# Query projection on tokens that are only scaled, with the shift's part as a product of its own, in a diffusion layer

## The chip, the cores and the metric

One core of one Trainium2 chip. The metric is the time of one execution in device microseconds, as the median of several runs.

## What is computed

One layer for 384 tokens of width 2048 in float32: 128 context tokens and 256 tokens of a denoising step, each group with its own conditioning vector. Cut to what matters here:

```python
mod = jax.nn.silu(cond) @ p['w_ada'][l] + p['b_ada'][l]           # 2048 x 12288
sh1, sc1, gt1, sh2, sc2, gt2 = jnp.split(mod[:, None, :], 6, axis=-1)
h = _rmsnorm(x, p['g_pre_mix'][l]) * (1.0 + sc1) + sh1
proj = h @ p['w_in'][l]                    # q, k, v, g, lr and the Hyena columns
...                                        # gated linear attention and Hyena, w_out, norm, gate
x = x + gt1 * _rmsnorm(y, p['g_post_mix'][l])
h = _rmsnorm(x, p['g_pre_ffn'][l]) * (1.0 + sc2) + sh2
y = _moe(h, l, p)                          # 16 experts, two for a token
```

`w_ada` is 100 MB. Its first third holds the shift `sh1` and the scale `sc1` that the first projection needs; the other four parts are wanted later.

## The kernel before, in words

All engines run programs written out by hand and tied by semaphores. `take` gives a PSUM bank to a result once the readers of the last one are done, `filled`, `read` and `freed` are its semaphores.

**Loads.** The SP engine issues one DMA for each entry of the list `loads` (L991 to L1002), in order: first sixteen 2 MB blocks of w_ada (128 rows by 4096 columns, shift and scale together), then the halves of w_in and w_out. A block goes into one of three ring slots, from the 17th load on into one of two; before it is issued, SP waits until TensorE has released the slot (`slot_done`). After each load SP issues so many *pieces* of the rest of w_ada (`PIECES_AFTER`, L367), 0.5 MB each as two DMAs, in a ring of four; piece n waits until VectorE has used piece n - 4 (L986). SP works strictly in order, so a load stands behind the pieces ahead of it. The rows of small vectors and the constants are issued by SP behind the first load (L968), the filter MLP's inputs and x by ScalarE's queue (L1215 to L1224), biases, gains, and later the lr and decay weights, masks and filter weights by GpSimd (L1076 to L1102, held at L1083 until the first tile is modulated).

**Start.** TensorE (L411 to L485) turns the small rows, does the first filter product (it waits for the MLP's inputs, L419), then sixteen `ada_step`s (L439), one for each block: eight products of 32 columns of weights by 512, four side by side in the array. Between the last eight it transposes the normalised tokens (`x_turn`, L456), which ScalarE copies into `hT` (L1256). When both sums are there, VectorE adds biases and gains (`mod_row`, L1557), TensorE transposes the two rows (`mod_columns`, L475), and VectorE modulates the 16 tiles of `hT` in 32 operations (L1623).

**Projections.** `project_half` (L487) takes one ring slot (8 row blocks by 512 columns of w_in) and does 8 products for each of 4 or 3 banks. Query (L526) comes first, 64 products of 384 columns, recorded in halves (x128); then the small lr product (L530), the eight decay products (L538), the key (L543), two value and two gate blocks, then six Hyena blocks. The four gated heads of the attention (`gla_head`, L596) are mixed into the second g1 half and the first Hyena blocks.

**The rest of w_ada.** VectorE sums the pieces, weighted by silu(cond), into 16 chunks (`ada_steps`, L1573). `run(n)` does n steps of two operations each; a piece is two steps, a chunk eight pieces. VectorE's program places these steps between its other work. TensorE then sums a chunk over partitions (`ada_sum`, L423, at the places of `ADA_SUMS`, L364), waiting for `chunk_ready`, and VectorE adds it (`mod_chunk`).

## Time and profile before

| what | value |
|---|---|
| median of 3 runs | 1532.09 us (1527.59 to 1532.54) |
| profiled execution, its own time | 1530.56 us |
| its span | 1528.7 us |
| mean granted TensorE clock | 0.965 |
| TensorE products busy | 1379.7 us (90%) |
| VectorE busy | 748.8 us (49%) |
| ScalarE busy | 241.7 us (16%) |
| HBM read and written | 408 MB and 23 MB, 282 GB/s over the span |

The span is the part between the first and the last instruction that the profiler saw; the difference to the execution's own time lies around it. Busy shares are averages over stages with different limits, so the views by stage and the chain of waits are read beside them. A granted clock of 1.00 is 2.4 GHz, 0.50 is 1.2 GHz.

### The profile page before, as it was taken

The numbers are of one execution on the slowest core, as the hardware profiler recorded it, in microseconds if no ns is written. First come the engines' busy times: TensorE is split into PE (matmuls) and PEld (weight loads), VectorE is DVE, ScalarE is ACT, GpSimd is POOL, SyncE is SP. The second block draws the span as 40 slices with busy tenths as digits, with TensorE's granted clock in tenths as the row PEclk, the third lists the DMA queues.
The fourth block names the chain that finished last, engine by engine and source line by source line (L and its number), as shares of the span: only waits on it lengthen the run. The fifth ranks groups of instructions, "written<-read, shape, count | busy, mean of one in ns | idle before, by whom it ended". The sixth has DMA issues, their size and how long they took to land.

```text
span 1528.7 us, 14045 instructions
## 1 busy us (share of the span) xinstructions
PE 1379.7 (90%) x5198; PEld 630.9 (41%) x5198; DVE 748.8 (49%) x1269; ACT 241.7 (16%) x401; POOL 75.1 (5%) x126
## 2 busy tenths in 40 slices
PE   2679999999999989999999999889989888798977
PEld 0135544444555545555544444543333333333322
DVE  0139889998677687978693752530000000000006
ACT  2110320100011111211121101521111101111104
POOL 3010000000001000000000001000000000000001
PEclk9689999999999999999999999989999999999999
DMA  9998458777549643322215844589999999999996
GB/s 345 424 359 254 170 173 276 249 259 254 165 144 339 222 146 109 117 69 90 83 55 213 289 157 170 235 351 427 427 426 394 430 427 428 426 386 427 427 424 279
DMA packets 134032, 422.19 MB, mean 276 GB/s; under 512 B 10253, under 2 KB 76024, under 8 KB 116852
## 3 DMA queue, kind: packets, MB, share of 16 engines
q1 hardware_dynamic: 120292, 375.79, 64.3%
q0 software_dynamic: 7584, 33.38, 6.0%
q10 hardware_dynamic: 6096, 12.20, 2.2%
q8 instruction: 40, 0.66, 0.2%
q14 instruction: 20, 0.16, 0.0%
HBM read 407.96 MB, written 22.58 MB: 282 GB/s over the span
## 4 chain that ended last, share of the span: by engine, by line
PE 74%; DMA 11%; DVE 8%; issue 3%; ACT 2%; ACTq 0%; POOL 0%; DVEq 0%; SPq 0%; POOLq 0%
PE ps L503 19%; PE ps L506 19%; PE ps L892 13%; PE ps L912 7%; DMA s_mem<-in_w_exp_gate 4%; PE ps L777 3%; DMA s_mem<-in_w_ada 3%; DMA s_mem<-in_w_exp_down 2%; DVE s_mem L1766 2%; PE ps L450 2%; PE ps L674 1%; DMA s_mem<-in_hy_freq 1%; PE ps L625 1%; PE ps L432 1%; DVE s_mem L1738 1%
## 5 line engine op out<-in xcount | busy, mean ns | idle before, releaser
L1592 DVE SCALAR_TENSOR_TENSOR s_mem<-s_mem,s_sT 128x512 f32<-128x512 f32 x480 | 339.4, 748 | 32.6 <-DMA s_mem<-in_w_ada 16.2
L503 PE MATMUL ps<-s_mem 128*128 128x384 f32 x1024 | 342.5, 492 | 1.1 <-DVE s_mem L1623 1.1
L506 PE MATMUL ps<-s_mem 128*128 128x512 f32 x672 | 292.8, 594 | 0.7 <-ACT s_mem L1366 0.7
L892 PE MATMUL ps<-s_mem 128*64 128x512 f32 x1152 | 256.4, 602 | 19.9 <-DMA s_mem<-in_w_exp_gate 18.7
L503 PEld LDWEIGHTS ps<-s_mem 128*128 128x128 f32 x1024 | 193.3, 191 | 142.5 <-issue 18.0
L506 PEld LDWEIGHTS ps<-s_mem 128*128 128x128 f32 x672 | 126.3, 190 | 158.5 <-issue 157.6
L892 PEld LDWEIGHTS ps<-s_mem 128*64 128x64 f32 x1152 | 87.4, 139 | 185.9 <-issue 185.9
L2059 DVE TENSOR_TENSOR s_mem<-s_mem,ps 64x512 f32<-64x512 f32 x18 | 12.2, 679 | 296.3 <-ACT s_mem L1461 296.3
L912 PE MATMUL ps<-s_mem 128*64 128x512 f32 x576 | 144.2, 659 | 9.3 <-DVE s_mem L2061 9.3
L1262 ACT ACTIVATE s_mem<-ps 128x512 f32<-128x512 f32 (+1 forms) x61 | 34.4, 581 | 316.3 <-PE ps L506 154.0
L912 PEld LDWEIGHTS ps<-s_mem 128*64 128x64 f32 x576 | 43.7, 150 | 96.4 <-issue 84.6
L2066 DVE COPY s_mem<-ps 128x512 f32<-128x512 f32 x18 | 12.4, 691 | 141.9 <-PE ps L912 141.9
L450 PE MATMUL ps<-s_mem,s_sT 128*32 128x512 f32 x256 | 43.2, 815 | 20.5 <-DMA s_mem<-in_w_ada 20.5
L1461 ACT ACT_TABLE_LOAD x17 | 21.8, 1283 | 241.0 <-PE ps L892 241.0
L625 PE MATMUL ps<-s_mem 128*128 128x512 f32 x96 | 42.9, 596 | 0.7 <-ACT s_mem L1262 0.7
L777 PE MATMUL ps<-s_mem 128*128 128x512 f32 x96 | 41.5, 592 | 0.0
L902 PE MATMUL ps<-s_base,s_mem 64*128 64x64 f32 x72 | 11.9, 285 | 30.9 <-DVE s_mem L2059 30.9
L1466 ACT ACTIVATE s_mem<-ps 128x512 f32<-128x512 f32 x18 | 10.7, 596 | 155.1 <-PE ps L912 155.1
L1307 ACT ACTIVATE s_mem<-ps,s_colB 128x384 f32<-128x384 f32 x24 | 16.1, 670 | 118.5 <-PE ps L503 118.5
L1893 DVE TENSOR_TENSOR s_mem<-s_mem,ps 128x512 f32<-128x512 f32 x12 | 7.9, 684 | 48.0 <-PE ps L777 25.1
L1347 ACT ACTIVATE s_mem<-s_mem 128x512 f32<-128x512 f32 x24 | 14.5, 630 | 93.5 <-DVE s_mem L1751 93.5
L450 PEld LDWEIGHTS ps<-s_mem,s_sT 128*32 128x32 f32 x256 | 8.3, 134 | 49.3 <-DMA s_mem<-in_w_ada 30.6
(287 smaller groups left out, 1025.0 us busy)
## 6 DMA issues: line engine op xcount, KB each, us to landing
s_mem<-in_w_ada SPq DMA_DIRECT2D x256, 256.0 KB, 3.2
s_mem<-in_w_exp_gate SPq DMA_DIRECT2D x32, 2048.0 KB, 21.1
s_mem<-in_w_exp_up SPq DMA_DIRECT2D x32, 2048.0 KB, 25.4
s_mem<-in_w_exp_down SPq DMA_DIRECT2D x32, 2048.0 KB, 24.4
s_mem<-in_w_in SPq DMA_DIRECT2D x24, 2048.0 KB, 8.8
s_mem<-in_w_ada SPq DMA_DIRECT2D x16, 2048.0 KB, 12.5
s_mem<-in_w_out SPq DMA_DIRECT2D x8, 2048.0 KB, 8.2
y_slots<-s_mem ACTq DMA_DIRECT2D x34, 256.0 KB, 11.1
```

Source lines behind the costliest of these rows:

```text
L450: m = mm(ps[32 * j:32 * j + 32, bank, :], sT[:, k, :], w[:, n, :], start=(k == 0), stop=(k == KT - 1), skip_group_check=True)
L503: m = mm(ps[:, banks[m_], 0:TOK], v[:, k, m_ * P:(m_ + 1) * P], hT[:, kk, :], start=(kk == 0), stop=(kk == KT - 1))
L506: m = mm(ps[:, banks[m_], :], hT[:, kk, m_ * P:(m_ + 1) * P], v[:, k, :], start=(kk == 0), stop=(kk == KT - 1))
L625: mm(ps[:, bank, :], dft[:, table, :], src, start=True, stop=True).then_inc(filled(key), 1)
L777: m = mm(ps[:, bank, :], hT[:, kh * 8 + k, t * P:(t + 1) * P], last_w[kh][:, k, :], start=(kh + k == 0), stop=(kh * 8 + k == KT - 1))
L892: m = mm(ps[half, 0, :], hgT[:, kh * 8 + k, :], weights(e, 2 * kh + which)[:, k, :], start=(kh + k == 0), stop=(kh * 8 + k == KT - 1), ski ...
L912: m = mm(ps[half, 4 + n // 2, :], heT[:, 2 * kh + k, :], weights(e, 4 + kh)[:, k, n * NCOL:(n + 1) * NCOL], start=(kh + k == 0), stop=(kh ...
L1262: a.op(A(dst, ps[:, b, 0:n], func), freed("act", key))
L1307: a.op(A(hyT[:, m_, :], ps[:, b, 0:TOK], ACT.Identity, bias=colB[:, 72 + c:73 + c], scale=colB[:, 24 + c:25 + c]), freed("act", key))
L1461: A(sg, ps[BLK:2 * BLK, 0, :], ACT.Silu).then_inc(S("sg_ready"), 1)
L1592: v.op(ve.scalar_tensor_tensor(out=o, in0=w, scalar=scale, in1=o, op0=ALU.mult, op1=ALU.add), S("piece_used") if last else None)
L1766: v.op(ve.reciprocal(temps[4 + s], ps[:, b, :]), freed("dve", f"norm{ho}{s}"))
```

## The change

w_ada's first third is now loaded in sixteen blocks of 256 rows by 2048 columns: eight for the scale, then eight for the shift. After the scale, VectorE only multiplies the tiles of `hT`, and TensorE does the query products on these scaled tiles between the shift's steps. The two query blocks of w_in have places of their own (`wq`) and are issued by SP behind the 9th and 12th load, no longer through the ring, which has two slots from the 9th load on. The shift's part of the query is 16 small products of the shift vectors with the same weights (`qshift`), turned into columns by four products (`colQ`), and added by ScalarE as the bias when it copies the query out (8 copies instead of 4, placed between the decay copies). VectorE adds the shift to `hT` in 32 more operations before the lr product.

Around this: seven pieces are issued between the shift's loads, 14 steps of `run` stand before the shift row and 4 behind the additions, where 26 stood behind the modulation; 2 more stand before the gated heads and 2 more in each of the heads 0, 1 and 3. The small vectors' rows and x go first on ScalarE's queue; the convolution rows are turned after the first scale step and the first filter product waits behind the fourth. GpSimd's loads are held until the first tile is scaled. Chunk 0 is summed after the first key half, chunk 8 after the first Hyena half.

```diff
+            shifts[32 * j + 2 + c, c] = 1
...
+        wq = [at(AT_ARENA + 2 * MIX + 1024, 8, NCOL), at(AT_ARENA, 8, NCOL)]
+        q_shift = at(AT_ARENA + 1536, NCOL)
...
-            slot = i % RING if i < KT else (i - KT + 1) % 2
+            slot = i % RING if i < 8 else i % 2
...
+        ADA_KEYS = ["ada0", "ada1"]
+        ADA_BANKS = [6, 7]
+        SHIFT, SCALE = 0, 1
+        Q_LOAD_AFTER = {8: 0, 11: 1}
         CHUNKS, PIECES = 16, 8
-        ADA_SUMS = {("q", 1): 0, ("k", 1): 1, ("v0", 1): 2, ("v1", 0): 3, ("v1", 1): 4, ("g0", 0): 5, ("g0", 1): 6,
-                    ("g1", 0): 7, ("g1", 1): 8, ("hy00", 1): 9, ("hy01", 1): 10, ("hy10", 0): 12,
+        ADA_SUMS = {("k", 0): 0, ("k", 1): 1, ("v0", 1): 2, ("v1", 0): 3, ("v1", 1): 4, ("g0", 0): 5, ("g0", 1): 6,
+                    ("g1", 0): 7, ("hy00", 0): 8, ("hy00", 1): 9, ("hy01", 1): 10, ("hy10", 0): 12,
                     ("wo1", 0): 13, ("wo2", 0): 14, ("wo2", 1): 15}
-        PIECES_AFTER = {1: 8, 2: 8, 3: 3, 4: 6, 5: 4, 6: 7, 7: 7, 8: 8, 9: 9, 10: 7, 11: 5, 12: 4, 13: 6, 14: 4,
-                        15: 6, 16: 4, 17: 8, 18: 2, 20: 2, 22: 2, 24: 2, 25: 4, 27: 4, 28: 6, 29: 2}
+        PIECES_AFTER = {9: 2, 10: 1, 11: 1, 12: 1, 13: 1, 14: 1, 15: 1, 16: 4, 17: 3, 18: 6, 19: 4, 20: 7, 21: 7, 22: 8,
+                        23: 9, 24: 8, 25: 6, 26: 5, 27: 6, 28: 4, 29: 7, 30: 4, 31: 8, 32: 2, 34: 2, 36: 2, 38: 2,
+                        39: 4, 41: 4, 42: 6, 43: 2}
         assert sum(PIECES_AFTER.values()) == CHUNKS * PIECES
...
-            def ada_step():
...
-                w = next_slot(pe, w_ada[k * P:(k + 1) * P, third * SLOT:(third + 1) * SLOT])
...
+            def ada_step(q, a):
+                w = next_slot(pe, w_ada[2 * a * P:2 * (a + 1) * P, q * D:(q + 1) * D].rearrange("(k p) n -> p k n", p=P))
+                bank, key = ADA_BANKS[q], ADA_KEYS[q]
+                if a == 0:
+                    take(pe, bank, key)
+                for k in (2 * a, 2 * a + 1):
+                    for j in range(4):
+                        m = mm(ps[32 * j:32 * j + 32, bank, :], sT[:, k, :], w[:, 4 * (k % 2) + j, :], start=(k == 0),
+                               stop=(k == KT - 1), skip_group_check=True)
                 slot_done(m, key if k == KT - 1 else None)
...
-            pe.wait_ge(S("sT_ready"), 2)
-            for k in range(KT):
-                ada_step()
-                if k == KT - 8:
-                    pe.wait_ge(S("hid_ready"), 1)
-                    take(pe, 3, "hid2")
-                    mm(ps[:, 3, 0:TOK], w2s, ftmp[0:HID, 1, :], start=True, stop=True).then_inc(filled("hid2"), 1)
-                    pe.wait_ge(S("x_scaled"), NT)
-                if KT - 8 <= k < KT - 1:
-                    for kt in range(3 * (k - KT + 8), min(KT, 3 * (k - KT + 8) + 3)):
-                        x_turn(kt)
+            def q_products(m_, kts):
+                for kt in kts:
+                    if m_ == 0:
+                        pe.wait_ge(S("h_scaled"), kt + 1)
+                    m = mm(ps[:, m_, 0:TOK], wq[kt // 8][:, kt % 8, m_ * P:(m_ + 1) * P], hT[:, kt, :],
+                           start=(kt == 0), stop=(kt == KT - 1))
+                return m
...
-            wait_read(pe, "dve", ADA_KEYS[0])
-            mod_columns(0, 2)
+            pe.wait_ge(S("sT_ready"), 2)
+            ada_step(SCALE, 0)
+            pe.wait_ge(S("in_rowsB"), 32)
+            take(pe, 4, "colB")
+            tr(ps[:, 4, 0:96], rowsB, ident[0:96, 0:96]).then_inc(filled("colB"), 1)
+            for a in (1, 2, 3):
+                ada_step(SCALE, a)
+            pe.wait_ge(S("in_mlp"), 16 * 9)
+            take(pe, 4, "hid1")
+            mm(ps[0:HID, 4, 0:TOK], w1s, pe_sb, start=True, stop=True).then_inc(filled("hid1"), 1)
+            pe.wait_ge(S("x_scaled"), NT)
+            for a in (4, 5, 6, 7):
+                ada_step(SCALE, a)
+                for kt in range(4 * (a - 4), 4 * (a - 3)):
+                    x_turn(kt)
             pe.wait_ge(S("mod_ready"), 1)
-            mod_columns(1, 3)
+            mod_columns(SCALE, 5)
+            pe.wait_ge(S("hid_ready"), 1)
+            take(pe, 4, "hid2")
+            mm(ps[:, 4, 0:TOK], w2s, ftmp[0:HID, 1, :], start=True, stop=True).then_inc(filled("hid2"), 1)
+            ada_step(SHIFT, 0)
+            pe.wait_ge(S("in_q0"), 16)
+            for m_ in range(4):
+                take(pe, m_, f"q_{m_}", ("act",))
+                m = q_products(m_, range(8))
+                if m_ == 3:
+                    m.then_inc(S("q_read"), 1)
+                ada_step(SHIFT, m_ + 1)
+            ada_step(SHIFT, 5)
+            pe.wait_ge(S("in_q1"), 16)
+            for m_ in range(4):
+                m = q_products(m_, range(8, 12))
+            m.then_inc(S("q_read"), 1)
+            ada_step(SHIFT, 6)
+            ada_step(SHIFT, 7)
+            for m_ in range(4):
+                if m_ == 2:
+                    wait_read(pe, "dve", ADA_KEYS[SHIFT])
+                    mod_columns(SHIFT, 5)
+                q_products(m_, range(12, KT)).then_inc(filled(f"q_{m_}"), 1)
+            wait_read(pe, "dve", "modT0")
+            take(pe, 6, "qshift", ("act",))
+            for k in range(KT):
+                j = k % 4
+                m = mm(ps[32 * j:32 * j + 32, 6, :], sT[:, k, :], wq[k // 8][:, k % 8, :], start=(k < 4),
+                       stop=(k >= KT - 4), skip_group_check=True)
+            m.then_inc(filled("qshift"), 1)
...
-            project("q", "fm", w_in, COL_Q)
+            pe.wait_ge(S("h_shifted"), KT)
...
+            wait_read(pe, "act", "qshift")
+            take(pe, 6, "colQ", ("act",))
+            for m_ in range(4):
+                m = mm(ps[:, 6, m_ * 32:m_ * 32 + 32], q_shift[:, m_ * P:(m_ + 1) * P], shift_rows, start=True, stop=True,
+                       skip_group_check=True)
+            m.then_inc(filled("colQ"), 1)
...
+            def load_q(kh):
+                if kh == 0:
+                    sp.wait_ge(S("x_scaled"), NT)
+                else:
+                    sp.wait_ge(filled(f"xT{KT - 1}"), uses[f"xT{KT - 1}"][2])
+                sp.dma_start(wq[kh], w_block(w_in, kh * 8 * P, COL_Q)).then_inc(S(f"in_q{kh}"), 16)
...
                 if i == 0:
-                    small_loads()
-                for _ in range(PIECES_AFTER.get(i - KT, 0)):
+                    sp.dma_start(base[:, :], T["k_base"]).then_inc(S("in_base"), 16)
+                if i in Q_LOAD_AFTER:
+                    load_q(Q_LOAD_AFTER[i])
+                for _ in range(PIECES_AFTER.get(i, 0)):
                     load_piece()
...
-            pool.wait_ge(S("h_modulated"), 1)
+            pool.wait_ge(S("h_scaled"), 1)
...
+            for rows, src in ((slice(0, 16), T["c_ctx"]), (slice(16, 32), T["c"][0]), (slice(32, 40), T["g_hy"][0]),
+                              (slice(40, 42), T["g_gla"][0]), (slice(42, 46), T["b_dec_f"][0]),
+                              (slice(46, 50), T["b_dec_b"][0])):
+                load(rowsA[rows, :], src.rearrange("(k p) -> k p", p=P), "in_rowsA")
+            for t in range(NT):
+                load(x_sb[:, t, :], x_rows[t], "in_x")
...
+            copy_out("qshift", q_shift)
             copy_out("lr", lrT)
+            b = read(act, "colQ")
+            a.op(A(colQ[:, :, :], ps[:, b, 0:4 * 32].rearrange("p (m n) -> p m n", n=32)[:, :, 0:2], ACT.Copy),
+                 freed("act", "colQ"))
+            a.sync()
+            def q_out(m_):
+                b = read(act, f"q_{m_}")
+                for c, toks in ((0, slice(0, SEQ)), (1, slice(SEQ, TOK))):
+                    a.op(A(qf[:, m_, toks], ps[:, b, toks], ACT.Identity, bias=colQ[:, m_, c:c + 1]),
+                         freed("act", f"q_{m_}") if c == 1 else None)
             for d in range(2):
                 for h in range(HEADS):
+                    if h % 2 == 0:
+                        q_out(2 * d + h // 2)
...
             inverse_roots(0, NT)
             for t in range(NT):
                 v.op(ve.tensor_scalar(h_tm[:, t, :], x_sb[:, t, :], stat[:, t:t + 1], None, ALU.mult), S("x_scaled"))
-            sine_argument("hid2", 1, P)
-            mod_row(0)
-            mod_row(1)
+            dve.wait_ge(S("in_mlp"), 16 * 9)
+            sine_argument("hid1", 0, HID)
...
-            mod_columns(0, 0)
-            mod_columns(1, 1)
+            mod_row(SCALE)
+            mod_columns(SCALE, 1)
             v.sync()
-            wait_read(dve, "act", f"xT{KT - 1}")
+            both = ((0, slice(0, SEQ)), (1, slice(SEQ, TOK)))
             for kt in range(KT):
-                for c, toks in ((0, slice(0, SEQ)), (1, slice(SEQ, TOK))):
-                    v.op(ve.tensor_scalar(hT[:, kt, toks], hT[:, kt, toks], modT[:, 1, c, kt:kt + 1],
-                                          modT[:, 0, c, kt:kt + 1], ALU.mult, ALU.add),
-                         S("h_modulated") if c == 1 else None)
-            run(26)
+                wait_read(dve, "act", f"xT{kt}")
+                for c, toks in both:
+                    v.op(ve.tensor_scalar(hT[:, kt, toks], hT[:, kt, toks], modT[:, 1, c, kt:kt + 1], None, ALU.mult),
+                         S("h_scaled") if c == 1 else None)
+            sine_argument("hid2", 1, P)
+            run(14)
+            mod_row(SHIFT)
+            b = read(dve, "modT0")
+            v.op(ve.tensor_copy(sT[:, :, 2:4].rearrange("p (j m) c -> p c j m", j=4),
+                                ps[:, b, :].rearrange("p (m j r) -> p r j m", m=4, j=4)[:, 0:2, :, :]),
+                 freed("dve", "modT0"))
+            v.sync()
+            for kt in range(KT):
+                if kt in (0, 8):
+                    dve.wait_ge(S("q_read"), kt // 8 + 1)
+                if kt == 12:
+                    dve.wait_ge(filled("q_3"), uses["q_3"][2])
+                for c, toks in both:
+                    v.op(ve.tensor_scalar(hT[:, kt, toks], hT[:, kt, toks], sT[:, kt, 2 + c:3 + c], None, ALU.add),
+                         S("h_shifted") if c == 1 else None)
+            run(4)
...
-            run(4)
+            run(6)
...
-                    run((2, 1, 2, 1, 1, 1, 2, 2)[event])
+                    run((2, 2, 2, 2, 1, 1, 2, 2)[event])
...
+            gla_head(1)
             mod_chunk(8)
-            gla_head(1)
```

## Rows read from the trace of the kernel before

**Rows 1.** the profile's page: the 40 slices, each 38 us wide
```profile
PE   2679999999999989999999999889989888798977
...
PEclk9689999999999999999999999989999999999999
DMA  9998458777549643322215844589999999999996
GB/s 345 424 359 254 170 173 276 249 259 254 165 144 339 222 146 109 117 69 90 83 55 213 289 157 170 235 351 427 427 426 394 430 427 428 426 386 427 427 424 279
```

**Rows 2.** the chain of waits from 60 to 210 us: start us, us, what
```profile
84.89 13.95 DMA s_mem<-in_w_ada
...
105.83 43.15 PE ps L503 x128
...
161.90 41.28 PE ps L503 x128
```

**Rows 3.** TensorE's timeline, 0 to 150 us: start, us, engine, line, what
```profile
57.88 3.61 PE L450 MATMUL ps<-s_mem,s_sT 128*32 128x512 f32 x16 [1.10 <-DMA s_mem<-in_w_ada]
...
75.98 1.92 PE L450 MATMUL ps<-s_mem,s_sT 128*32 128x512 f32 x16
...
98.89 3.59 PE L450 MATMUL ps<-s_mem,s_sT 128*32 128x512 f32 x16 [3.11 <-DMA s_mem<-in_w_ada]
...
104.09 0.66 PE L479 MATMUL ps<-s_base,s_mem 128*128 128x128 f32 x4 [1.03 <-DVE s_mem L1568]
```

**Rows 4.** five stretches: us, busy us of each engine, granted clock, DMA share, GB/s
```profile
26.00:34.00 8.00, 7.62 (x49) 1.78 (x48) 2.83 (x6) 3.23 (x4) 0.00 (x0) 1.00 0.86 330
36.00:56.00 20.00, 10.86 (x64) 2.09 (x64) 3.85 (x4) 4.19 (x5) 0.00 (x0) 0.71 1.01 430
56.00:98.00 42.00, 29.70 (x182) 9.87 (x178) 2.87 (x6) 7.75 (x17) 0.00 (x0) 0.81 0.99 414
112.00:124.00 12.00, 12.00 (x39) 7.05 (x38) 11.15 (x23) 0.00 (x0) 1.33 (x3) 1.00 1.01 271
128.00:140.00 12.00, 12.00 (x39) 7.07 (x38) 10.91 (x17) 0.98 (x2) 0.00 (x0) 1.00 1.02 342
```

**Rows 5.** DMA queues from 105 to 125 us: packets, MB, share of 16 engines
```profile
q0 software_dynamic: 480, 0.92, 17.8%
```

**Rows 6.** VectorE's timeline at the modulation
```profile
102.62 0.69 DVE L1562 TENSOR_TENSOR s_mem<-s_mem,ps 128x512 f32<-128x512 f32 x1 [0.98 <-PE ps L450]
...
105.01 9.87 DVE L1623 TENSOR_SCALAR s_mem<-s_mem,s_modT 128x128 f32<-128x128 f32 x32
```

**Rows 7.** the timeline of all engines, lr and decay products, 148 to 163 us
```profile
149.37 0.52 PE L532 MATMUL ps<-s_mem 128*32 128x384 f32 x2
...
156.55 1.23 ACT L1271 ACTIVATE s_mem<-ps,s_colA 128x384 f32<-128x384 f32 x2 [1.15 <-PE ps L541]
...
161.74 1.45 PE L503 MATMUL ps<-s_mem 128*128 128x384 f32 x4
```

**Rows 8.** VectorE's timeline, chunk sums up to the first gated head
```profile
348.98 0.89 DVE L1587 TENSOR_SCALAR s_mem<-s_mem,s_sT 128x512 f32<-128x512 f32 x2 [0.23 <-DVE s_mem L1592]
...
354.84 2.87 DVE L1592 SCALAR_TENSOR_TENSOR s_mem<-s_mem,s_sT 128x512 f32<-128x512 f32 x4
358.77 2.87 DVE L1592 SCALAR_TENSOR_TENSOR s_mem<-s_mem,s_sT 128x512 f32<-128x512 f32 x4 [1.07 <-DMA s_mem<-in_w_ada]
361.67 0.42 DVE L1554 TENSOR_TENSOR s_mem<-s_mem,ps 64x256 f32<-64x256 f32 x1
```

**Rows 9.** TensorE's timeline, the sum of chunk 7
```profile
358.91 1.06 PE L432 MATMUL ps<-s_mem 128*32 128x256 f32 x8
```

**Rows 10.** the stretch of the first gated head, columns as in rows 4
```profile
358.00:392.00 34.00, 34.00 (x125) 15.42 (x125) 23.29 (x44) 2.74 (x7) 1.08 (x2) 1.00 0.57 181
```

More of the change, by code:

```diff
@@ L77, in shape_constants @@
     lower = (np.arange(P) >= BLK)[:, None]
-    base = np.concatenate([ident, tri, sel.reshape(P, 2 * P), total, np.tile(rows, (P, 1)), tokens, lower], 1).astype(np.float32)
+    shifts = np.zeros((P, 32), np.float32)
+    for j in range(4):
+        for c in range(2):
+            shifts[32 * j + 2 + c, c] = 1
+    base = np.concatenate([ident, tri, sel.reshape(P, 2 * P), total, np.tile(rows, (P, 1)), tokens, lower, shifts], 1).astype(np.float32)
     masks = np.zeros((P, 2, P), np.int32)
@@ L154, in build @@
         gain = mem[:, AT_GAIN:MEM].rearrange("p (q n) -> p q n", q=4)
-        base = sb("base", [P, 4 * P + 32 + N_ROWS + NT + 1])
+        base = sb("base", [P, 4 * P + 32 + N_ROWS + NT + 1 + 32])
+        colQ = sb("colQ", [P, 4, 2])
         masks = sb("masks", [P, 2, P], I32)
@@ L435, in ada_sum @@
                 mi.then_inc(filled(key), 1)
-            ada_at = [0]
-            def ada_step():
-                third, k = divmod(ada_at[0], KT)
-                ada_at[0] += 1
-                w = next_slot(pe, w_ada[k * P:(k + 1) * P, third * SLOT:(third + 1) * SLOT])
-                for n in range(8):
-                    bank, j = ADA_BANK + n // 4, n % 4
-                    key = ADA_KEYS[third * 2 + n // 4]
-                    if k == 0 and j == 0:
-                        take(pe, bank, key)
-                    m = mm(ps[32 * j:32 * j + 32, bank, :], sT[:, k, :], w[:, n, :], start=(k == 0),
-                           stop=(k == KT - 1), skip_group_check=True)
-                    if k == KT - 1 and n == 3:
-                        m.then_inc(filled(key), 1)
+            def ada_step(q, a):
[4 more added lines that the diff above has]
+                for k in (2 * a, 2 * a + 1):
+                    for j in range(4):
+                        m = mm(ps[32 * j:32 * j + 32, bank, :], sT[:, k, :], w[:, 4 * (k % 2) + j, :], start=(k == 0),
+                               stop=(k == KT - 1), skip_group_check=True)
                 slot_done(m, key if k == KT - 1 else None)
@@ L499, in project_half @@
                         kk = kh * 8 + k
-                        if key == "q" and m_ == 0:
-                            pe.wait_ge(S("h_modulated"), kk + 1)
                         if kind == "fm":
@@ L1222, in _ @@
                 load(dst, src, "in_mlp")
-            for t in range(NT):
-                load(x_sb[:, t, :], x_rows[t], "in_x")
             wait_read(act, "dve", "colA")
```

33 lines of the change are left out of this document (7 added, 26 removed).

## The prediction

> **What bounds the kernel now.** I read the page's 40 slices first [rows 1]. The slices are 38 us wide. In the first three DMA stands at 9 tenths, TensorE at 2, 6 and 7 tenths and the granted clock dips to 6 and 8 tenths; from the fourth on TensorE is full. So the start of this kernel is bound by DMA, the rest up to the experts by TensorE. The chain of waits says the same with names [rows 2]: a w_ada load up to 98.8 us, then the whole query projection (43.15 us), later the key projection (41.28 us). No query product runs while w_ada loads, although the step waits show that TensorE needs 1.92 us (full clock) or 3.6 us (half) for what a load brings each 4.9 us [rows 3]. The thing to be won is TensorE's idle time before 99 us.
>
> Each microsecond by which the key projection starts sooner (161.7 us now [rows 7]) reaches the end only if the work beside it keeps up. That is VectorE's weighted sum of the other 16 chunks of w_ada, in 256 steps of `run`.
>
> **When the last shift load lands.** A 2 MB (2.097 MB) load at 430 GB/s (36:56 in [rows 4]) takes 4.9 us.
> - The eighth load was there at 57.9 us [rows 3] (the first row is the eighth step). DMA had a hole in 26:34, 330 instead of 430 GB/s over 8 us [rows 4], 1.9 us, because the ring waited behind the filter MLP's inputs. The change moves that wait behind the fourth step. I take 55.7 us; bounds 54 (the small transfers no longer in the way at all) and 57.9 (no gain).
> - Eight more loads: 39.2 us.
> - Two w_in loads, moved forward past eight w_ada loads on SP's queue: between 4.9 us (430 GB/s) and 6.1 us (342 GB/s, the stretch 128:140 where w_in and pieces mix [rows 4]); I take 5.2, nearer to whole loads: 10.4 us.
> - Seven pieces (0.524 MB each) are issued on SP's queue before the last load, none before in that stretch: 1.53 us each at 342 GB/s, bounds 1.2 (430) and 1.9 (271, 112:124 in [rows 4]): 10.7 us.
> - GpSimd's queue waits for the first scaled tile instead of the first modulated one, so lr weights, decay weights, masks and w3 come some 40 us sooner, into the full stretch. Their queue took 17.8% of 20 us [rows 5], 3.6 us; bound 0 if they fall into a gap.
>
> Sum: 55.7 + 39.2 + 10.4 + 10.7 + 3.6 = 119.6 us, where the last w_ada load is there at 98.9 now. Bounds 111.4 and 126.2. A transfer later to the last load is the price of the change.
>
> **When the last step ends.** TensorE does the scale steps, transposes, and between shift steps 0 to 4 the first 32 query products, 8 at a time: 8 x 0.645 us (41.28 us / 64 products [rows 2]) = 5.2 us, plus 1.9 for the step, against a load with piece or w_in of 6.4 to 11.6 us. They hide behind DMA and cost nothing; 1.3 us apiece at half clock, 10.3 + 3.6 us, they would not. VectorE's scaling (32 operations, 9.87 us [rows 6], 0.62 us a tile, the products' own pace) begins some 5 us after the eighth load and ends near 71 us. Then come its 14 steps of chunk sums (28 operations of 0.72 us [rows 8], 20 us); the last of their 7 pieces is issued behind the seventh shift load and is there at about 114 us, so they end before the last shift step.
>
> Behind shift step 5 stand 16 products and two steps. That load is there at 119.6 - 2 x 4.9 - 2 x 1.53 = 106.7 us. It follows idle time, so I take the step at 3.6 us, as after the wait before 98.89 [rows 3]; then 16 x 0.645 = 10.3 us and 2 x 1.92: E = 124.4 us. By DMA alone it would be 119.6 + 1.9 = 121.5, so here TensorE binds. Bounds: 115.3 (early loads, full clock) and 130.3 (late ones).
>
> **From there to the lr product.** 8 products 5.2 us (VectorE's shift row, 0.7 us [rows 6], lies beside them), four transposes to the start of the additions 0.9 us (104.09 to 105.01 now [rows 3, 6]), 32 additions 9.9 us: lr starts at E + 16.0 = 140.4 us. TensorE's own way, 16 products, the transposes and the 16 new shift products (two steps' worth, 3.84 us), ends at E + 14.8 and is hidden by the additions. lr starts at 149.4 now [rows 7]: 9.0 us gained.
>
> **From lr to the key projection.** The four colQ products and ScalarE's small copy: 0.3 us on the path. The eight query copies with bias replace four plain ones and stand between the decay copies; ScalarE idles 1.15 us before a pair [rows 7], and two copies of 128 and 256 columns should need some 0.7 us, where one of 384 takes 0.6 [rows 7]. I cost them at nothing; without that cover 4 x 0.7 = 2.8 us. Chunk 0's sum moves from the query into the key projection: + 1.0 us (1.06, [rows 9]), since lr no longer has it ahead.
>
> **The stall behind it.** VectorE has done 14 + 4 steps before the decay's, 26 + 4 before: 8 steps, 11.7 us, less. Until the gated heads nothing gives this back, and ScalarE's exponentials tie VectorE to the key projection's end. So counted from that point each chunk is ready as late as the one 8 steps further is now. Chunk 7 is ready at 348.8 now, and at the place of 361.6 then [rows 8]; TensorE wants it at 358.9 [rows 9]. Earlier chunks just fit. That is 2.7 us, TensorE waiting in the sum before the second half of g1, with everything behind it. Chunk 8's sum moves half a projection on and has room. Three of the four heads get 2 steps more (2.9 us each) and pay back 6; VectorE is busy 23.3 of 34 us in the first [rows 10], so I cost these at nothing, at most 3 x 2.9 = 8.7 us.
>
> Sum: -9.0 + 0.3 + 1.0 + 2.7 = **-5.0 us**. The rest is the same program and starts sooner by as much, the experts' weights too. The profiled execution took 1530.56 us (span 1528.7), 1.5 below the median of 1532.09: 1525.6.
>
> **Rivals.**
> 1. *Early* (0.18). GpSimd's transfers fall into gaps (-3.6), step 5 meets a full clock (-1.7) and loads are 0.7 sooner: E = 118.4, 1519.6 us. For it: 414 GB/s sustained even now [rows 4]. Against: the mixed stretch at 271.
> 2. *The load queue eats it* (0.19). Pieces at 1.9, w_in at 6.1 us, no gain at the start: E near 130, nothing left, 1531.
> 3. *Slower: half clock where it binds* (0.08). The granted clock is 0.71 in 36:56 and 0.81 in 56:98 with TensorE half to two thirds busy [rows 4], that is, both levels, 1.2 and 2.4 GHz, alternate. If from shift step 5 to E the lower one is granted throughout, the stretch takes 3.6 + 20.6 + 7.2 = 31.4 instead of 17.7 us: +13.7, 1539.3 us. It decides from some 5 us of such delay on, a third of the stretch. Against: the query projection now starts behind the same kind of waits and loses only 43.15 - 41.28 = 1.9 us [rows 2]. The Trainium skill (TensorE: Matmul & The Clock Gate, "HAM oscillation") has a matmul kernel whose loads leave it idle fall back to the half clock at each tile; by that rule this rival is the likely one. The trace agrees for single steps (3.6 us after a wait), but not for a run of products.
> 4. *VectorE's debt comes due in the heads* (0.06): +8.7, 1534.3 us. Against: its 10.7 us idle in the first head.
>
> The forecast keeps 0.49. Its own range is 1521.5 to 1530. Case 3 and the edge of 2 set the top of the range; case 1 and the lower bound of E (-9) the bottom: 1516 to 1536.
>
> **Chances.** What a measurement of this kernel tells from no change is 0.3%, 4.6 us: below 1527.5 is faster. The forecast is 1.9 us beyond it, so two thirds of its 0.49 count as faster, with all of case 1: 0.50. Case 2, 4 and the forecast's rest: 0.36 within. Case 3 and the tails of 2 and 4: 0.14.
>
> **What would show it.** Right: last shift step ends at 122 to 127 us; lr starts 16 us later behind VectorE's additions; the key projection starts at 153; DMA at 9 tenths up to 120; TensorE waits some 3 us for VectorE before the second half of g1. Wrong: a shift step that waits for VectorE's pieces on SP's queue; x or the convolution rows landing so late on ScalarE's queue that the second scale step (which now waits for them) holds the ring; E beyond 129; any wait over 2 us in the heads; the experts not starting sooner by what the key projection and the stall leave.

## The result and the profile after

The changed kernel took 1533.18 us (median of 19 executions, 1530.58 to 1537.98), the one before 1529.59 in 19 executions of the same set: ratio 1.0025, interval 1.0016 to 1.0034. In a second set, twelve executions of the same change, it was 1.0007 (0.9996 to 1.0019). No gain, then, and at most a third of a per cent lost. I had forecast 1525.6, a gain. 1533.18 lies within the whole range I gave (1516 to 1536), above the forecast's own (1521.5 to 1530), and on the other side of no change.

The profile's page of the changed kernel, the lines that answer to [rows 1]:

```profile
span 1531.0 us, 14163 instructions
...
PE   3679999999999989999999999889989887898887
...
PEclk9899999999999999999999999989999999999999
DMA  9996558877549743322215844499999999999996
GB/s 362 379 393 212 172 168 274 270 236 263 181 138 344 236 144 103 125 69 90 83 55 211 292 156 169 206 378 428 426 427 395 426 427 428 427 394 425 428 415 275
```

The first slices look much as before: TensorE at 3, 6 and 7 tenths, DMA at 9. The rate, though, is 379 GB/s in the second slice, where it was 424. TensorE's timeline of the changed kernel says what that does (start us, us, engine, line, what, and in brackets the idle time before it and what ended it):

```profile
28.94 0.42 PE L479 MATMUL ps<-s_base,s_mem 96*128 96x96 f32 x1 [11.56 <-DMA s_mem<-in_hy_conv_b]
...
56.26 1.92 PE L448 MATMUL ps<-s_mem,s_sT 128*32 128x512 f32 x16 [1.03 <-DMA s_mem<-in_w_ada]
...
71.19 8.05 PE L464 MATMUL ps<-s_mem 128*128 128x384 f32 x16 [6.10 <-DMA s_mem<-in_w_in]
...
105.81 1.92 PE L448 MATMUL ps<-s_mem,s_sT 128*32 128x512 f32 x16 [3.85 <-DMA s_mem<-in_w_ada]
112.39 3.64 PE L448 MATMUL ps<-s_mem,s_sT 128*32 128x512 f32 x16 [4.66 <-DMA s_mem<-in_w_ada]
115.97 11.32 PE L464 MATMUL ps<-s_mem 128*128 128x384 f32 x32
127.21 3.64 PE L448 MATMUL ps<-s_mem,s_sT 128*32 128x512 f32 x32
130.78 5.43 PE L464 MATMUL ps<-s_mem 128*128 128x384 f32 x16
...
145.20 2.76 PE L567 MATMUL ps<-s_mem 128*32 128x384 f32 x32
...
157.40 7.90 PE L539 MATMUL ps<-s_mem 128*128 128x384 f32 x24
```

L448 is a step, L464 the query products (two records a product), L567 lr, L539 the key projection. Shift step 5 starts at 112.4 us, the last step ends at 130.85 (E), lr starts at 145.2 and the key projection at 157.4, 4.3 us sooner than in [rows 7]. VectorE's timeline beside it:

```profile
120.14 2.86 DVE L1645 SCALAR_TENSOR_TENSOR s_mem<-s_mem,s_sT 128x512 f32<-128x512 f32 x4 [3.47 <-DMA s_mem<-in_w_ada]
130.99 0.69 DVE L1615 TENSOR_TENSOR s_mem<-s_mem,ps 128x512 f32<-128x512 f32 x1 [7.99 <-PE ps L448]
136.69 0.21 DVE L1683 COPY s_sT<-ps 128x32 f32<-128x32 f32 x1 [5.01 <-PE ps L472]
136.93 7.42 DVE L1693 TENSOR_SCALAR s_mem<-s_mem,s_sT 128x128 f32<-128x128 f32 x32
```

The 32 additions take 7.42 us, not the 9.87 of [rows 6]: an operation with one arithmetic step where that had two. VectorE stands idle 7.99 us for the last step, so its chunk sums are not what is late. Further on, TensorE of the changed kernel around the sum of chunk 7, then windows of the same place (stretch, us, busy us of PE, PEld, DVE, ACT, POOL, granted clock, DMA share, GB/s):

```profile
358.29 1.06 PE L435 MATMUL ps<-s_mem 128*32 128x256 f32 x8 [2.46 <-DVEq L1649]
...
359.27 4.54 PE L542 MATMUL ps<-s_mem 128*128 128x512 f32 x6
...
364.38 2.84 PE L542 MATMUL ps<-s_mem 128*128 128x512 f32 x6
```

```profile
359.30:361.00 1.70, 1.70 (x5) 0.93 (x4) 1.66 (x3) 0.00 (x0) 0.00 (x0) 0.65 0.98 322
361.00:363.00 2.00, 2.00 (x3) 0.68 (x2) 0.50 (x2) 0.00 (x0) 0.00 (x0) 0.50 0.53 139
```

The stall is there (2.46 us before L435), and the six records behind it ran at half clock: 4.54 instead of 2.84 us.

How the lead shrinks, start in the changed kernel less start before: lr -4.2, key projection -4.3, chunk 6 -3.15 (333.97 against 337.12), chunk 7 -0.6 (358.29, [rows 9]), chunk 9 +1.1 (457.69 against 456.61), first expert product +1.8 (1015.13 against 1013.37), span +2.3. So the start gave half of what was forecast (4.3 of 8.6 us at the key projection), the way from there to the experts cost 6.1 us, where I had counted 3.7, and another 0.5 us was lost behind the first expert product, which no run explains.

### The profile page after: what moved, and what is told of

It reads as the page before. It is cut to its first block, busy times and chain, and to the rows that moved or that the text cites. A ratio compares the mean times of both kernels' runs of the same rounds, so it can differ in the third digit from the quotient of the medians.

```text
span 1531.0 us, 14163 instructions
## 1 busy us (share of the span) xinstructions
PE 1380.4 (90%) x5238; PEld 633.5 (41%) x5238; DVE 754.1 (49%) x1301; ACT 242.9 (16%) x407; POOL 74.7 (5%) x126
## 4 chain that ended last, share of the span: by engine, by line
PE 62%; DMA 16%; DVE 15%; issue 3%; ACT 2%; SPq 1%; ACTq 0%; POOL 0%; DVEq 0%; POOLq 0%
PE ps L539 16%; PE ps L933 13%; PE ps L542 10%; PE ps L953 7%; DVE s_mem L1645 7%; DMA s_mem<-in_w_ada 6%; DMA s_mem<-in_w_exp_gate 6%; PE ps L818 3%; PE ps L464 2%; DVE s_mem L1835 2%; DMA s_mem<-in_hy_conv_b 2%; PE ps L715 1%; PE ps L448 1%; PE ps L666 1%; DMA y_slots<-s_mem 1%
## 5 line engine op out<-in xcount | busy, mean ns | idle before, releaser
L539 PE MATMUL ps<-s_mem 128*128 128x384 f32 x896 | 299.6, 491 | 0.0
L933 PE MATMUL ps<-s_mem 128*64 128x512 f32 x1152 | 256.6, 602 | 18.9 <-DMA s_mem<-in_w_exp_gate 17.7
L539 PEld LDWEIGHTS ps<-s_mem 128*128 128x128 f32 x896 | 168.2, 191 | 123.8 <-issue 16.2
L2128 DVE TENSOR_TENSOR s_mem<-s_mem,ps 64x512 f32<-64x512 f32 x18 | 12.2, 680 | 295.4 <-ACT s_mem L1517 295.4
L448 PE MATMUL ps<-s_mem,s_sT 128*32 128x512 f32 x256 | 35.7, 687 | 18.3 <-DMA s_mem<-in_w_ada 17.6
L464 PE MATMUL ps<-s_mem 128*128 128x384 f32 x128 | 46.4, 520 | 6.1 <-DMA s_mem<-in_w_in 6.1
L818 PE MATMUL ps<-s_mem 128*128 128x512 f32 x96 | 41.5, 592 | 0.0
L464 PEld LDWEIGHTS ps<-s_mem 128*128 128x128 f32 x128 | 25.4, 203 | 28.8 <-issue 8.0
```

What stands on the lines that cost most here:

```text
L448: m = mm(ps[32 * j:32 * j + 32, bank, :], sT[:, k, :], w[:, 4 * (k % 2) + j, :], start=(k == 0), stop=(k == KT - 1), skip_group_check=True)
L464: m = mm(ps[:, m_, 0:TOK], wq[kt // 8][:, kt % 8, m_ * P:(m_ + 1) * P], hT[:, kt, :], start=(kt == 0), stop=(kt == KT - 1))
L539: m = mm(ps[:, banks[m_], 0:TOK], v[:, k, m_ * P:(m_ + 1) * P], hT[:, kk, :], start=(kk == 0), stop=(kk == KT - 1))
L818: m = mm(ps[:, bank, :], hT[:, kh * 8 + k, t * P:(t + 1) * P], last_w[kh][:, k, :], start=(kh + k == 0), stop=(kh * 8 + k == KT - 1))
L933: m = mm(ps[half, 0, :], hgT[:, kh * 8 + k, :], weights(e, 2 * kh + which)[:, k, :], start=(kh + k == 0), stop=(kh * 8 + k == KT - 1), ski ...
```

## The experiments

The theory: the load queue is late by more than I priced, and what the start still wins is eaten behind the key projection, above all by chunk 7. Rivals: TensorE binds before E, by the 16 products behind step 5; VectorE's debt moves elsewhere if the sum is moved; pieces and GpSimd's loads cost nothing because they fall into gaps. No edit leaves out any of the computation unless it says so. One profile was taken of each; "step 5", "E", "lr" and "key" are read in it as above.

**Twice the same code.** First, how far one profile of the start can be trusted.

> The changed kernel once more, unaltered: how far profiled executions of one program differ in the start. If the time of shift step 5 (112.4 us in its first profile, 110.1 in the experiment whose start is the same code) is the program's own, it is between 110 and 113 again; the ratio to the kernel before is 1.0025 +- 0.001.

Ratio 1.0007 (0.9996 to 1.0019). TensorE's timeline of this second profile:

```profile
74.95 1.92 PE L448 MATMUL ps<-s_mem,s_sT 128*32 128x512 f32 x16 [0.43 <-DMA s_mem<-in_w_ada]
...
85.55 3.62 PE L448 MATMUL ps<-s_mem,s_sT 128*32 128x512 f32 x16 [3.32 <-DMA s_mem<-in_w_ada]
...
110.40 3.64 PE L448 MATMUL ps<-s_mem,s_sT 128*32 128x512 f32 x16 [4.56 <-DMA s_mem<-in_w_ada]
```

Step 5 at 110.4 instead of 112.4, E at 129.3. The late-sum kernel below has the same code up to here and shows 110.1 and 127.4. So from one profile to the next step 5 scatters by 2.3 us, E and the key projection by 3.5, and I compare others with the mean of the three: **step 5 at 110.95, E at 129.2, key at 155.7**.

**Chunk 7's sum half a projection later.**

```diff
-                    ("g1", 0): 7, ("hy00", 0): 8, ...
+                    ("g1", 1): 7, ("hy00", 0): 8, ...
...
-            mod_chunk(7)
             gla_head(0)
+            mod_chunk(7)
             gla_head(1)
```

> Chunk 7 is summed after the second half of g1 instead of the first, and added by VectorE behind the first gated head. Theory A (the gain of the overlap is given back where TensorE waits for chunk 7, 2.5 us, and then runs at half clock for a while, 1.7 us): both vanish, the second g1 half starts some 2.5 us sooner, its first six products take 2.8 instead of 4.5 us, and the kernel is 4.2 us faster than the change, about 0.4 us under the kernel before. Rival B (VectorE's debt only moves to the next place where TensorE needs it): the wait shows up at a later sum or in the heads, and the gain is under 1.5 us. Rival C (the half clock has nothing to do with the wait): 2.5 us are won, 1.7 stay.

1529.71 us, ratio 1.0001 (0.9991 to 1.0010). The stall is gone, and this stands in its place (TensorE's timeline of this kernel):

```profile
339.46 13.04 PE L542 MATMUL ps<-s_mem 128*128 128x512 f32 x30
353.63 2.84 PE L542 MATMUL ps<-s_mem 128*128 128x512 f32 x6 [1.13 <-DMA s_mem<-in_w_in]
```

The second half of g1 now waits 1.13 us for its weights, and there is no half clock behind so short a wait. In [rows 9] and in the changed kernel nothing waited for that load. The next limit stood close behind the first. From the key projection to chunk 9's sum this kernel takes 297.7 us, the change 300.3 and 298.9 in its two profiles: the move is worth 1.1 to 2.6 us, not the 4.2 expected.

**GpSimd's loads late.**

```diff
-            pool.wait_ge(S("h_scaled"), 1)
+            pool.wait_ge(S("q_read"), 2)
```

> GpSimd's loads (lr and decay weights, masks) are held until the twelfth tile's products are done instead of the first scaled tile, so that they lie behind the shift's loads. Theory A (every byte on the DMA engines ahead of the last shift load counts): shift step 5 starts 3 to 4 us sooner than 112.4 us, and the end of the last shift step moves as much. Rival D (their packets fall into gaps): no change within 1 us at step 5. If they land too late for the lr product, that product waits and the whole is slower.

1526.61 us, ratio 0.9979 (0.9969 to 0.9989); step 5 at 106.6, E at 125.1. The DMA queues in 66:86, first of the changed kernel, then of this one (queue: packets, MB, share of 16 engines):

```profile
DMA packets 2651, 6.93 MB, mean 346 GB/s; under 512 B 315, under 2 KB 1778, under 8 KB 2113
...
q1 hardware_dynamic: 2169, 5.99, 88.0%
q0 software_dynamic: 480, 0.92, 15.5%
```

```profile
DMA packets 2584, 8.07 MB, mean 403 GB/s; under 512 B 157, under 2 KB 1693, under 8 KB 1825
...
q1 hardware_dynamic: 2582, 8.05, 102.9%
```

With the same 480 packets out of the way SP's queue moves 8.05 MB instead of 5.99. By share GpSimd's queue took 3.1 us (15.5% of 20); by what SP's queue lost it is 2.06 MB at 403 GB/s, 5.1 us. Step 5 came 3.9 us sooner over the two profiles that have this edit (106.6 and 107.5). Two other profiles with the change's own loads have 5.98 and 6.02 MB in this window, so the 2.06 MB are no scatter. So they do not fall into gaps: rival 1 of the prediction had it wrong, and my 3.6 us was at the low end of 3.9 to 5.1.

**All 16 products ahead of shift step 5.**

```diff
-            ada_step(SHIFT, 5)
             pe.wait_ge(S("in_q1"), 16)
             for m_ in range(4):
                 m = q_products(m_, range(8, 12))
             m.then_inc(S("q_read"), 1)
+            ada_step(SHIFT, 5)
             ada_step(SHIFT, 6)
```

> The 16 products of tiles 8 to 11 stand ahead of shift step 5 instead of behind it. Theory E (TensorE binds between step 5 and the last step, with 16 products whose inputs were there before): they fill the 8.5 us in which it waits for steps 4 and 5 now; the last shift step ends near 125 instead of 130.9 us, bound by the last load, and the kernel is 5 to 6 us faster than the change. Rival F (DMA binds there anyway, the last load being late by itself): the last step ends at 129 or later and under 2 us are won.

1533.52 us, ratio 1.0024 (1.0012 to 1.0036): nothing won. TensorE's timeline of this kernel, and below it SP's, whose rows are the issues of loads:

```profile
106.32 11.61 PE L464 MATMUL ps<-s_mem 128*128 128x384 f32 x32
117.86 3.64 PE L448 MATMUL ps<-s_mem,s_sT 128*32 128x512 f32 x32
127.30 3.64 PE L448 MATMUL ps<-s_mem,s_sT 128*32 128x512 f32 x16 [5.80 <-DMA s_mem<-in_w_ada]
```

```profile
119.84 0.37 SPq L1038 DMA_DIRECT2D s_mem<-in_w_ada  x1
```

The last load shares its slot with step 5's. Step 5 released it at 119.8, behind the products, and the load landed 7.4 us after its issue. In the changed kernel as it was SP issued it at 116.1, it landed 9.0 us later, at 125.1, and lay there unused until TensorE was done with the steps and products ahead of it, near 129. The rival "TensorE binds, so move its work" falls in this form: TensorE's work sets when the slot comes free, and the load comes back as the wait. The prediction's sum knew only one of the two.

**No pieces between the shift's loads.** All 18 chunk-sum steps moved behind the decay product.

```diff
-        PIECES_AFTER = {9: 2, 10: 1, 11: 1, 12: 1, 13: 1, 14: 1, 15: 1, 16: 4, 17: 3, ...
+        PIECES_AFTER = {15: 4, 16: 8, 17: 3, ...
...
-            run(14)
             mod_row(SHIFT)
...
-            run(4)
...
-            run(4)
+            run(22)
```

> The seven pieces among the shift's loads are issued behind the last one, and VectorE's 14 steps stand behind the decay products. Only the stretch up to the lr product is to be read; behind it VectorE owes 14 more steps and the whole is slower, by some 10 us or more. Theory A: at my price of 1.5 us a piece step 5 starts 7.7 us sooner (five pieces ahead of it); if pieces are what I mispriced, 10 us or more. Rival D: pieces cost next to nothing, and step 5 moves by under 3 us.

One execution, 1542.87 us, span 1541.1. Step 5 at 103.4, 7.6 us sooner for five pieces: 1.5 us each, as I had priced them. E at 121.0 and the key projection at 147.6, that is, at the start 14 us are won over the kernel before. Windows of this kernel show the queue's rate with fewer kinds of transfer about: in 84:92 a w_in block with its 2 KB rows is under way (1175 packets), in 92:100 w_ada blocks alone (441 packets).

```profile
84.00:92.00 8.00, 8.00 (x44) 3.37 (x32) 0.00 (x0) 0.00 (x0) 0.00 (x0) 1.00 1.03 395
92.00:100.00 8.00, 7.05 (x36) 3.38 (x32) 0.00 (x0) 0.00 (x0) 0.00 (x0) 1.00 1.02 424
```

Alone, 2 MB loads in 8 KB rows move at 424 GB/s, nearly the 430 I had taken; beside w_in's rows it is 395, at full DMA share in both. Then TensorE's timeline:

```profile
172.29 1.92 PE L435 MATMUL ps<-s_mem 128*32 128x256 f32 x8 [3.92 <-DVEq L1649]
183.65 23.48 PE L539 MATMUL ps<-s_mem 128*128 128x384 f32 x64 [9.44 <-DMA s_mem<-in_w_in]
210.23 1.92 PE L435 MATMUL ps<-s_mem 128*32 128x256 f32 x8 [3.10 <-DVEq L1649]
```

16.5 us of waits follow at once, two on VectorE's sums and one on a w_in load that stands behind pieces on SP's queue, and the experts start at 1024.9, 11.6 us later than before. The pieces have to be paid somewhere; between the shift's loads they were cheap.

**The two moves together, and half of the products ahead of step 5.** The first joins the edits of the late sum and the late GpSimd loads. The second moves step 5 in between the 16 products:

```diff
-            ada_step(SHIFT, 5)
             pe.wait_ge(S("in_q1"), 16)
             for m_ in range(4):
+                if m_ == 2:
+                    ada_step(SHIFT, 5)
                 m = q_products(m_, range(8, 12))
```

> GpSimd's loads behind the shift's loads and chunk 7's sum half a projection later, both. Alone they gave about 7.0 and 3.7 us against the change. Theory A (the two costs lie one behind the other on TensorE's path): they add up, 1533.2 - 10.7 = 1522.5 us, 0.4 to 0.5% under the kernel before. Rival B (both only paid down the same debt, so that VectorE is late next wherever TensorE comes sooner): 7 us at most, 1526.

> Of the 16 products of tiles 8 to 11 eight stand ahead of shift step 5 and eight behind it. Before, all 16 ahead of it brought nothing: step 5 then ended 4 us later, and since the last load waits for its ring slot, it was issued later and the last step waited 5.8 us for it. Theory G (the last step is set by step 5's end plus the last load's 8 us or plus the work behind step 5, whichever is longer): step 5 keeps its time, 10 us of work behind it become 5, and the last step ends near 125 us, 5 us sooner; the kernel is some 4 us faster than the change. Rival H (VectorE or the sums behind eat whatever comes sooner): under 1.5 us.

The joined edits: 1526.56 us, 0.9975 (0.9965 to 0.9984), against 0.9979 with GpSimd's alone. They do not add up: the profile again shows a wait for g1's weights, 1.31 us at 352.7, and no stall. Half of the products early: 1530.99 us, 1.0000 (0.9987 to 1.0014), E at 127.5, although step 4 started later than in the changed kernel (106.2 against 105.8). From step 4 to E it needs 21.3 us, the three profiles of the change's own order 25.0, 25.4 and 23.8. The release of the slot is delayed by eight products instead of sixteen, and TensorE fills the wait for step 5's load. I had expected E near 125 and some 4 us against the change; E came 1.7 us before the mean of the three and level with the earliest of them (127.4), so it is the stretch from step 4 to E that shows the gain.

**All three.**

> All three: GpSimd's loads late, chunk 7's sum late, eight products ahead of shift step 5. Theory A and G: 4 us on top of the two, some 1519 us, 0.7% under the kernel before. Rival B: no better than the two, because VectorE's debt of 8 steps then shows at chunks 5 and 6 (0.2 and 2 us of room).

1522.64 us (six executions), ratio **0.9950** (0.9931 to 0.9969), faster than both kernels, though not the 1519 expected. And once more:

> The version with the late loads of GpSimd, the late sum of chunk 7 and half of the 16 products ahead of shift step 5 once more, unaltered. If its gain is real the ratio to the kernel before lies in 0.993 to 0.997 again, with the last shift step ending at 121 to 126 us in the profile. If it was a lucky set, 0.997 to 1.000 (each of its parts alone gave 0.9979 to 1.0001).

1524.31 us (six executions), 0.9957 (0.9936 to 0.9978). TensorE's timeline of this second profile:

```profile
100.90 1.92 PE L448 MATMUL ps<-s_mem,s_sT 128*32 128x512 f32 x16 [2.73 <-DMA s_mem<-in_w_ada]
102.75 5.43 PE L464 MATMUL ps<-s_mem 128*128 128x384 f32 x16
108.11 1.93 PE L448 MATMUL ps<-s_mem,s_sT 128*32 128x512 f32 x16
109.96 5.43 PE L464 MATMUL ps<-s_mem 128*128 128x384 f32 x16
115.32 1.92 PE L448 MATMUL ps<-s_mem,s_sT 128*32 128x512 f32 x16
120.34 3.48 PE L448 MATMUL ps<-s_mem,s_sT 128*32 128x512 f32 x16 [3.10 <-DMA s_mem<-in_w_ada]
```

No gap from 100.9 to 117.2 and full clock throughout; E is 123.8 (121.9 in the first profile), the key projection starts at 150.5 (148.4). That is 11.3 and 13.3 us before [rows 7], of which 5.7 and 8.2 reach the experts.

How much of this is the third edit's is not shown. From step 4 to E the two profiles need 22.9 and 22.8 us, those with GpSimd's loads late and the products in the change's order 24.9 and 25.4: some 2 us, as above. But at chunk 12's sum the two lead the kernel before by 6.4 and 9.0 us, GpSimd's late loads alone by 7.1 and the two joined edits by 5.6, and in the stretch behind it the latter two lose 2.5 us to a half clock that the former two do not meet (last section). What these medians gain over 0.9979 and 0.9975 may be that stretch as well as the split.

**Is it the rows?** Two things in the new start have shorter rows than the loads of before: w_ada's blocks (8 KB instead of 16) and the query's (2 KB). Both were replaced by loads of the same bytes in 16 KB rows from w_ada. The layer's result is then another (scale, shift or query), and with it the experts' work, so the times of the whole (one execution each, 1533.19, 1555.72 and 1557.47 us) say nothing, and the start alone is compared.

```diff
-                sp.dma_start(wq[kh], w_block(w_in, kh * 8 * P, COL_Q)).then_inc(S(f"in_q{kh}"), 16)
+                sp.dma_start(wq[kh], w_ada[kh * P:(kh + 1) * P, SLOT:2 * SLOT].rearrange("p (k n) -> p k n", n=NCOL)).then_inc(S(f"in_q{kh}"), 16)
```

```diff
-                w = next_slot(pe, w_ada[2 * a * P:2 * (a + 1) * P, q * D:(q + 1) * D].rearrange("(k p) n -> p k n", p=P))
+                w = next_slot(pe, w_ada[(8 * q + a) * P:(8 * q + a + 1) * P, 0:SLOT])
```

> The two query blocks are loaded from w_ada, 128 rows of 16 KB, in place of 1024 rows of 2 KB from w_in; the bytes are the same, the query that comes out is another, so only the part up to the key projection is read. Three profiles of the unaltered order give 112.4, 110.4 and 110.1 us (with the late sum) for shift step 5. If the short rows are what makes the query loads dearer than the 5.2 us I priced (a stretch with such a load moves 336 to 378 GB/s instead of 410), two loads save 2 x 0.5 to 2 x 1.2 us: step 5 between 108.5 and 110. Rival, rows don't matter and the rate is that of a queue in which more than one kind of transfer waits: step 5 within 1 us of 111.

> All 16 w_ada blocks of the first third are loaded as 128 rows of 16 KB, as the kernel before does, instead of 256 rows of 8 KB; the shift and scale that come out are not the layer's, so only the part up to the key projection is read. Theory, shorter rows cost rate (411 instead of 430 GB/s, 0.23 us a load): the eighth step starts 1 to 2 us sooner than 56.3 and step 5 about 3 us sooner than 111, at 108. Rival, the 8 KB rows cost nothing and the loss comes from pieces, query loads and GpSimd's queue: both within 1 us of 56.4 and 111.

> Both alterations of the last two runs, with the same parts of the computation changed. If row length is the cause of both losses, step 5 comes near the 106.7 us of the prediction, at most 107.5; if neither is, it stays within 1 us of 111. In between, the difference to 111 is the share of row length and the rest is the pieces (1 KB rows) and GpSimd's loads, which this run leaves as they are.

| from the eighth step to step 5 | us |
|---|---|
| priced (55.7 to 106.7) | 51.0 |
| the change's own order, three profiles | 56.1, 53.8, 53.6 |
| query blocks in long rows | 53.3 |
| w_ada in long rows | 53.0 |
| both | 52.5 |

The order is as row length would have it, but two of the three unaltered values lie within 0.7 us of the single edits. In 86:106, windows of the changed kernel and of the one with long query rows:

```profile
86.00:106.00 20.00, 15.14 (x70) 6.91 (x72) 5.79 (x9) 0.00 (x0) 0.00 (x0) 1.00 1.04 400
```

```profile
86.00:106.00 20.00, 16.66 (x76) 6.89 (x68) 7.34 (x11) 0.00 (x0) 0.00 (x0) 0.93 1.02 413
```

400 and 413 GB/s, both below the 430 of [rows 4]. Row length explains 1 to 2 us at most; against the scatter of 2.5 us between the unaltered profiles these single ones do not settle it further. The wide w_ada rows showed something else instead. I expected the eighth step sooner and it came at 62.8, six us later, by TensorE's timeline because of this:

```profile
35.58 0.42 PE L479 MATMUL ps<-s_base,s_mem 96*128 96x96 f32 x1 [18.80 <-DMA s_mem<-in_hy_conv_b]
```

The convolution rows on ScalarE's queue land at 35.6 us instead of 28.9, and the scale steps behind them hold the ring: in 36:40 SP's queue moves nothing. The prediction had named just this as what could go wrong; with 8 KB rows it costs little, a share of 0.91 and 316 GB/s in 32:36 of the changed kernel. The Trainium skill (DMA: Bandwidth & Descriptors, "Queues, rings and completion order") has each DMA engine take turns between the queues with work, a whole packet from each; longer packets on SP's queue would then hold the small ones back. Both traces agree with that. The queues in 24:29, SP's and then ScalarE's (packets, MB, share), first of the changed kernel, then of this one:

```profile
q1 hardware_dynamic: 246, 1.90, 94.8%
q10 hardware_dynamic: 243, 0.05, 5.8%
```

```profile
q1 hardware_dynamic: 112, 1.57, 78.6%
q10 hardware_dynamic: 109, 0.43, 21.6%
```

Nearly one packet for one, and with packets of 14 instead of 7.7 KB on SP's queue fewer than half as many of ScalarE's get through.

## Why the prediction was wrong

**The failed step: the last shift load and, with it, E.** Forecast 124.4, measured 130.85, and 129.2 over three profiles: 4.8 us late. By terms:

| term | forecast | mean of three | off by |
|---|---|---|---|
| eighth step | 55.7 | 56.5 (56.3, 56.7, 56.5) | +0.8 |
| eighth step to step 5 | 51.0 | 54.5 | +3.5 |
| step 5 to E | 17.7 | 18.2 | +0.5 |
| E to lr | 16.0 | 14.35 | -1.65 |
| lr to key | 12.7 | 12.2 | -0.5 |
| key projection starts | 153.1 | 155.7 | +2.6 |

Within the 51.0 us the pieces were right (7.6 for five, priced at 7.65) and GpSimd's loads cost 3.9, by what SP's queue lost 5.1, priced at 3.6. What is left of the 3.5 us lies in the six w_ada and two w_in loads: without pieces 46.6 us from the eighth step to step 5, less 3.9, is 42.7 for 16.8 MB, 393 GB/s, where my 4.9 and 5.2 us came to 39.8: 2.9 us. With 5.1 for GpSimd's it is 41.5 us, 404 GB/s and 1.7 us; no run leaves out both the pieces and GpSimd's loads, so the division between them stays open. The step of the prediction that failed is "a 2 MB load at 430 GB/s", as the price of a load that does not run alone: I took the rate of the best stretch (36:56), in which one queue ran whole 16 KB-row loads, although the same group had 414 for the longer 56:98. w_ada blocks alone do move at 424 in 92:100 of the kernel without pieces. But the stretch the change fills has three kinds of transfer, and over 20 us SP's queue does not come back to that even without GpSimd's: 399 GB/s in 86:106 of the kernel with those loads late, at full DMA share. A ring that stands still is not the cause: in no window of 4 us between 56 and 112 is the DMA share of the changed kernel below 0.97.

**"Here TensorE binds" was half of it.** From step 5 to E it did take TensorE's 17.3 to 18.9 us. By the last load alone, there at 125.1, E would have been near 127 instead of 130.85. But moving all the products forward gained nothing, because the slot's release and the last load's 7.4 us then end as late. The sum had no term for the ring of two slots.

**E to lr**: I had lr wait for VectorE's additions. They took 2.45 us less than priced and ended at 144.35; what set lr's start was TensorE's own way, priced at E + 14.8 and 14.35 in all three profiles. **lr to the key projection**: ScalarE's eight copies with bias did hide, 0.73 us a pair; the colQ products were paid.

**The stall** was right: VectorE late for chunk 7, forecast 2.7 us, measured 2.46, 1.91, 1.86, 1.81 and 2.33 in the five profiles that keep the place and the layer's own loads. (That earlier chunks just fit was not so in all: chunk 4's sum waited 0.73, 0.29 and 0.71 us in three of them.) Not in the sum was what it sets off: 1.7 us of half clock behind the longer ones. Chunk 0's sum cost its 1.06 in the key projection as forecast. Of the heads, costed at nothing, one took 0.5 us more. Together that is 5.7 of the 6.1 us from key projection to experts, where 3.7 was forecast; 0.4 is unexplained.

**Against the rivals.** Rival 2, the load queue eats it, came closest in E ("near 130, nothing left, 1531"), but not by its own price for pieces: what was dearer was loads beside other transfers. The end is later than its 1531, in part by the clock behind the stall. Rival 1 (GpSimd's transfers in gaps, -3.6) is refuted. Rival 3, half clock from step 5 to E throughout, +13.7, did not come: the timeline has 3.64 us for step 5, then 11.32 for 16 products, priced at 10.3 at full clock. The Trainium skill (TensorE: Matmul & The Clock Gate, "HAM oscillation") has a matmul kernel whose clock falls at each wait for a load. Behind the waits of 4.66, 4.56 and 4.57 us for step 5 the traces agree: the step took 3.64, 3.64 and 3.24 us instead of 1.92. But it is that step and at most 1.5 us on the products behind it (10.59 to 11.75), and behind the wait of 3.85 us before step 4 the step took 1.92. Rival 4 did not come: no wait over 2 us in the heads. I gave 0.50 to faster and 0.36 to within 0.3%, and the median lies within it at +0.23%. The lead of 1.9 us over the bound was itself not there: the bound of 1527.5 stood on a median of three executions, 1532.09, where the 19 of the later set have 1529.59. With 0.3% below that, 1525.0, my 1525.6 is no gain clear of the noise, and one term of 3 us was enough to undo what was left.

## What to carry to other kernels

Price a stretch that is filled with mixed transfers at the rate of the nearest mixed stretch, and count for it all queues that feed it; here 393 to 404 instead of 430 GB/s on 17 MB was the larger part of the error before step 5, and holding 0.92 MB of another queue back for 60 us was worth 0.3 to 0.5% by itself. In a ring of two, work put ahead of the step that frees a slot delays a load by as much, so split such work around the step: all 16 products ahead won nothing, eight of them took 2 to 4 us off the stretch from step 4 to E. With the two other edits the whole came to 0.9950 and 0.9957. And a microsecond won at the start is worth only what the next engine's debt lets through: 11 to 13 us won before the key projection arrived as 6 to 8 at the experts.

## What had not been expected of the hardware

- Two queues cost more than their shares. GpSimd's 480 packets, 0.92 MB, took 15.5% of 20 us, and SP's queue moved 2.06 MB less in them: 346 instead of 403 GB/s in all.
- The length of a wait and the clock behind it. At the sum of chunk 7 a wait of 2.30, 2.33, 2.46, 2.50 or 2.89 us was followed by some 1.7 us of half clock in all five profiles that had it, one of 1.81, 1.86 or 1.91 in none of three. In the start it is not so plain: a wait of 3.85 us had no half clock behind it. What decides is open.
- A half-clock stretch that comes and goes. In 780:835 the granted clock was 1.00 in seven profiles, the one of before among them, and 0.94 in the seven others, and the way from chunk 12's to chunk 13's sum took 168.5 to 168.7 instead of 166.0 us. It begins among small transposes, between which TensorE waits 1.7, 0.2, 0.2 and 0.7 us for ScalarE, in both kinds of profile alike; in the kernel with half of the products early one group of them takes 1.54 us, in the second profile of the change 1.02, and the 48 records behind the last wait 22.97 and 20.87. I can put these 2.5 us on no edit's account; the two kernels that were profiled twice had 1.00 both times. The same stretch in the windows of the second profile of the change and of the kernel with half of the products early:

```profile
780.00:835.00 55.00, 52.21 (x138) 23.85 (x137) 35.85 (x56) 8.92 (x17) 1.61 (x3) 1.00 0.37 134
```

```profile
780.00:835.00 55.00, 52.25 (x132) 24.06 (x131) 35.26 (x55) 9.08 (x17) 1.61 (x3) 0.94 0.37 134
```

- VectorE's 32 operations on 128x128 and 128x256 tiles, half each, took 7.42 us with one arithmetic step (the additions) and 9.87 with two; the scaling, also one step, 8.14.
- Left open: why loads that move at 424 GB/s alone stay near 400 at full DMA share once other transfers are about, of which row length is at most a part; and what of the 2.3 us of scatter at step 5 belongs to which load.
